# A fp32 hybrid block on one core: the third norm's factor in every eviction of its projection, fewer writes of the normed residual, last projection's residual in two pieces

## The chip, the cores and the metric

One of the cores of one Trainium2 chip runs the whole program. The time is device microseconds (us) from the start to the end of one execution; the median of several executions counts. One execution of the kernel before was profiled, and all rows below come from it.

## What is computed (reference, cut)

A block with T = 512 positions and D = 1024 columns is followed by a second one. The change touches the second, whose middle part is this:

```python
def second_block(x, w_in, norm_g, pool_w, pool_scale, fox_bf, w_out, final_g):
    for layer in range(DEPTH):
        h = rmsnorm_2(x, norm_g[layer])
        z = jnp.einsum('bld,dc->blc', h, w_in[layer])
        (pv, pg, dq, dk, dv, dg, iq, ik, iw, fq, fk, fv, fg, ff) = split_columns(z)
        a_out = pool_mixer(pv, pool_w[layer], pool_scale[layer]) * jax.nn.silu(pg)
        b_o = dsa_mixer(dq..., dk..., dv..., iq..., ik, iw * idx_w_scale, topk)
        b_out = b_o.reshape(B, L, DSA_WIDTH) * jax.nn.silu(dg)
        log_f = jax.nn.log_sigmoid(ff.astype(jnp.float32) + fox_bf[layer].astype(jnp.float32))
        c_o = fox_mixer(fq..., fk..., fv..., log_f)
        c_out = c_o.reshape(B, L, FOX_WIDTH) * jax.nn.silu(fg)
        mixed = jnp.concatenate([a_out, b_out, c_out], axis=-1)
        x = x + jnp.einsum('blc,cd->bld', mixed, w_out[layer])
    return rmsnorm_2(x, final_g)
```

The norm multiplies each column by a gain and each position by one number, r(t). The projection is linear, so r(t) can be multiplied in before it, or after it at each result. The sparse attention (dsa) selects 128 keys per query by scores: eight indexer heads, each relu(iq . ik) times a weight. The forgetting attention (fox) needs the running sum of log f.

## The kernel before, in words

Everything is kept transposed: channels on the 128 partitions, the 512 positions along the row. A projection is a list of **units**. One unit is one block of 128 output columns over all of K = 1024. The fp32 product is made of three passes (high x high, low x high, high x low), so a unit is 8 x 3 = 24 matmuls of 128x512 into one bank of `gb` (four banks, unit u uses u % 4). Its weights arrive by a DMA of SP into `raw` (four buffers), ACT copies them to a rounded `whi` (line 1101), and DVE or POOL subtracts to get `wlo` (line 1494 or 2233). `whi` and `wlo` have two buffers. `split(n)` names this; `POOL_SPLITS` says for which n POOL does the subtraction.

The third stage is a projection of 31 units (`Z_UNITS`), numbered here 0 to 30: unit 0 "thin" (indexer key, indexer weights, forget gates), units 1 and 2 the indexer queries, then q, k, v, g of six head pairs ("groups"), and four units of the pooling mixer. Each engine's program walks these units, four quarters of six matmuls each, and after quarter m of unit u it does what `schedule()` has put at (u, m). Slot s means quarter s % 4 of unit s // 4. In the plan stand, in order of slots: `spread` (PE broadcasts the norm's row r(t) into `gd`, ACT copies it to SBUF), `turn_iw` (PE transposes unit 0's result, DVE takes the gates from it), `log_f` (ACT an exp, DVE a chain of 18 small instructions, each waiting for the one before: `log1p`, line 1499 and after), `cum_f`, `turn_f`, 24 `score` entries (PE one product with 32 rows, ACT relu into one of two buffers, DVE multiply-add into `selb`), 48 `round` entries (DVE max and replace, eight keys each), and for each group the attention steps `s`, `weigh`, `t`, `turn_v`, `pv`, `mix`, `low`.

Before unit 0 the residual in `act_a` is only multiplied by the gain ("raw"): r(t) is not known yet. `RAW_UNITS` = 4 units use this raw residual and get r(t) when DVE evicts them (lines 2035, 2037, 2044). For units 4 to 30 the entries `norm` make a second copy with r(t) in it: DVE eight products (line 1931), ACT eight copies (line 1409), POOL eight subtractions (line 2220). Units from 4 on wait for these by `z_hi` and `z_lo`, and their results are evicted by ACT (q, v, g, pv, pg; lines 1364 to 1386) or DVE (k, line 2046) without a factor. ACT takes the silu of a gate unit straight from PSUM.

All engines work through their own program in order. PE may run at most four banks ahead of evictions, two buffers ahead of splits, and two relu buffers ahead of DVE's scores.

The last projection (`W_ORDER`) has all of `gb` and `gd` as its output, two banks for each of four position tiles c. The residual is put in first as products with the identity (line 1073), for tiles 2, 3, 1, 0, then eight rows of weights follow (line 1086), 24 matmuls each. Tiles 0 and 1 lie in `gb` and may be overwritten only when the last pooled output has been read (`ot_ready` 8).

Of the kernel before, what the change touches and what calls it, by code (L numbers as in the profile page):

```python
# [5 lines left out]
P = 128  # L6
F32 = mybir.dt.float32
# [30 lines left out]
Z_HI, Z_LO = 2 * KD, 3 * KD  # L38
OUT_HI, OUT_LO = 0, KD
RAW_UNITS = 4  # L40
# [32 lines left out]
           + [(w, 0, c) for w, c in (("k", B_FK), ("q", B_FQ), ("v", B_FV), ("g", B_FG))]  # L73
           + [(w, g, c + g * P) for g in range(1, 3) for w, c in (("q", B_FQ), ("k", B_FK), ("v", B_FV), ("g", B_FG))]
# [26 lines left out]


def reads_of(what):
    return [count for (name, _, _), (_, count) in zip(Z_UNITS, Z_READER) if name == what]


Q_READ, K_READ, V_READ, G_READ, PV_READ, PG_READ = (reads_of(w) for w in ("q", "k", "v", "g", "pv", "pg"))


def schedule():  # L110
# [4 lines left out]
    put(1, 2, ("norm", 0))  # L115
    put(2, 0, ("turn_iw",))
    put(2, 1, ("spread", 3))
    put(2, 2, ("norm", 1))
# [4 lines left out]
    for n, (c, h) in enumerate(todo):  # L123
        put((14 + n * 10 // 24) // 4, (14 + n * 10 // 24) % 4, ("score", n, c, h))
# [7 lines left out]
    for g in range(GROUPS):  # L132
        start = 4 * 6 + 16 * g
# [9 lines left out]
        todo.setdefault(start + (7 if g < GROUPS - 1 else 10), []).append((2, ("turn_v", g)))  # L143
# [10 lines left out]
    assert max(todo) == 4 * last  # L154
# [30 lines left out]
def hybrid_block_kernel(nc, x, norm_mix_g, w_in, conv_a_w, gdn_conv_w, gdn_A_log, gdn_dt_bias, gdn_norm_g,  # L185
                        w_a_out, w_b_out, w_o, norm_ffn_g, w_up, ffn_conv_w, w_down, norm_final_g,
                        w_in_2, norm_g_2, pool_w_2, pool_scale_2, fox_bf_2, w_out_2, final_g_2, out):
    with ExitStack() as ctx:
# [109 lines left out]
        token_row, final_row = flat(ob), wk[:, 0:T]  # L298
        fresh = (qc[:], kc[:], vc[:], cx[:], ca[:], flat(LT), flat(AT), flat(Kt))
# [75 lines left out]
        klen_ready = sem("klen_ready")  # L375
        g_kept = sem("g_kept")
# [61 lines left out]
        z_read_v = sem("z_read_v")  # L438
# [52 lines left out]
        POOL_SPLITS = range(N_Z + 5, N_W)  # L491
# [12 lines left out]
        def _(sp):  # L504
# [49 lines left out]
            sp.wait_ge(cols_exp, 2)  # L554
# [62 lines left out]
        def _(pe):  # L617
# [1649 lines left out]
```

## Time and profile before

| | |
|---|---|
| median of 3 runs | 1375.5 us (1375.22 to 1379.77) |
| the profiled execution | 1378.33 us, its span 1376.6 us |
| mean granted TensorE clock over the span | 0.978 |
| busy, share of the span | PE 97%, DVE 60%, ACT 43%, POOL 19% |
| DMA | 113 MB, mean 82 GB/s |

Busy is the time an engine spends in instructions. PE's share says little by itself: a matmul at half clock is busy twice as long. The clock column (PEclk, 1.00 is 2.4 GHz and 0.50 is 1.2 GHz) has to be read beside it. The third stage runs from about 1024 us to 1315 us, the last projection from there to 1370 us.

### The profile page before, as it was taken

The numbers are of one execution on the slowest core, as the hardware profiler recorded it, in microseconds if no ns is written. First come the engines' busy times: TensorE is split into PE (matmuls) and PEld (weight loads), VectorE is DVE, ScalarE is ACT, GpSimd is POOL, SyncE is SP. The second block draws the span as 40 slices with busy tenths as digits, with TensorE's granted clock in tenths as the row PEclk, the third lists the DMA queues.
The fourth block names the chain that finished last, engine by engine and source line by source line (L and its number), as shares of the span: only waits on it lengthen the run. The fifth ranks groups of instructions, "written<-read, shape, count | busy, mean of one in ns | idle before, by whom it ended". The sixth has DMA issues, their size and how long they took to land.

```text
span 1376.6 us, 20315 instructions
## 1 busy us (share of the span) xinstructions
PE 1329.6 (97%) x6848; PEld 1054.3 (77%) x6848; DVE 820.3 (60%) x1685; ACT 588.4 (43%) x1015; POOL 266.6 (19%) x493
## 2 busy tenths in 40 slices
PE   6899999999999999999999999999996999999998
PEld 4788878888788788888788888788775567766676
DVE  4657676666676743345577753677675468873522
ACT  5345445364454432224344432344553255555412
POOL 1113033031230300002400000000134224643200
PEclk9999999999999999999999999999998599999999
DMA  5233232332332223333233233332342122222211
GB/s 157 63 85 85 77 84 76 84 84 69 91 84 72 81 78 92 93 105 92 86 99 100 82 92 107 99 99 75 86 115 64 35 58 62 66 74 62 62 54 69
DMA packets 209560, 113.34 MB, mean 82 GB/s; under 512 B 6954, under 2 KB 206953, under 8 KB 209513
## 3 DMA queue, kind: packets, MB, share of 16 engines
q1 hardware_dynamic: 209129, 112.72, 28.4%
q8 instruction: 26, 0.43, 0.1%
q14 instruction: 21, 0.17, 0.0%
q0 software_dynamic: 384, 0.03, 0.0%
HBM read 110.59 MB, written 2.11 MB: 82 GB/s over the span
## 4 chain that ended last, share of the span: by engine, by line
PE 93%; DVE 4%; ACT 2%; issue 1%; POOL 0%; DMA 0%; POOLq 0%; DVEq 0%; ACTq 0%
PE gb L634 76%; PE gd L1008 2%; PE gb L1086 2%; PE gd L1086 2%; PE gd L979 1%; PE gd L1021 1%; PE gd L1031 1%; PE gd L646 1%; DVE wlo L1494 1%; PE gd L707 1%; PE gd L719 1%; PE gd L811 1%; PE gd L802 0%; PE gb L1073 0%; PE gd L791 0%
## 5 line engine op out<-in xcount | busy, mean ns | idle before, releaser
L634 PE MATMUL gb<-act_a,whi 128*128 128x512 f32 x2800 | 958.8, 404 | 11.8 <-POOL selb L2209 5.0
L634 PEld LDWEIGHTS gb<-act_a,whi 128*128 128x128 f32 x2800 | 531.3, 190 | 141.1 <-issue 19.5
L634 PE MATMUL gb<-act_a,wlo 128*128 128x512 f32 x1488 | 585.3, 393 | 0.0
L1494 DVE TENSOR_TENSOR wlo<-raw,whi 128x1024 fp32r<-128x1024 f32 x186 | 232.3, 1249 | 159.0 <-ACT whi L1101 158.3
L1101 ACT ACTIVATE whi<-raw 128x1024 fp32r<-128x1024 f32 x212 | 224.1, 1057 | 234.6 <-PE gb L634 201.4
L634 PEld LDWEIGHTS gb<-act_a,wlo 128*128 128x128 f32 x1488 | 283.1, 190 | 52.6 <-issue 1.7
L634 PE MATMUL gb<-act_b,whi 128*128 128x512 f32 x304 | 109.2, 389 | 0.0
L2233 POOL TENSOR_TENSOR wlo<-raw,whi 128x1024 fp32r<-128x1024 f32 x26 | 62.8, 2416 | 138.1 <-ACT whi L1101 138.1
L634 PEld LDWEIGHTS gb<-act_b,whi 128*128 128x128 f32 x304 | 57.1, 188 | 11.9
L2199 POOL TENSOR_TENSOR zs<-zs,ca 128x512 f32<-128x512 f32 x3 | 4.4, 1457 | 314.3 <-ACT ca L1104 314.3
L2143 POOL TENSOR_TENSOR elt<-Ti,Ue 128x60 f32<-128x60 f32 (+14 forms) x120 | 44.1, 368 | 27.5 <-POOL Ue L2146 13.3
L2146 POOL TENSOR_TENSOR Ue<-Ue,elt 128x60 f32<-128x60 f32 (+14 forms) x120 | 39.5, 329 | 9.4
L1181 ACT ACTIVATE ob<-gd,hc 128x128 f32<-128x128 f32 x24 | 8.8, 367 | 58.2 <-DVE Rr L1692 58.2
L2171 POOL TENSOR_TENSOR zs<-zs,ca 128x512 f32<-128x512 f32 x3 | 5.6, 1857 | 134.8 <-ACT ca L1104 134.8
L2156 POOL TENSOR_TENSOR rr<-ss,rr 128x4 f32<-128x4 f32 x8 | 1.6, 200 | 152.7 <-DVE ss L1711 152.7
L2150 POOL TENSOR_TENSOR rr<-ss,eps_one 128x4 f32<-128x4 f32 x8 | 2.1, 263 | 142.9 <-DVE ss L1647 142.9
L1873 DVE TENSOR_TENSOR Yb<-gb,Vt 128x512 f32<-128x512 f32 x22 | 15.2, 691 | 23.2 <-PE gb L634 23.2
L1983 DVE MAX8 small<-selb 128x8 f32<-128x256 f32 (+2 forms) x48 | 26.7, 556 | 0.7
L1231 ACT ACTIVATE act_a<-ca 128x512 f32 (+1 forms) x8 | 5.1, 632 | 50.8 <-DVE ca L1758 50.8
L1984 DVE MATCH_REPLACE8 selb<-small,selb 128x256 f32<-128x256 f32 (+2 forms) x48 | 26.1, 543 | 0.0
L634 PE MATMUL gb<-act_b,wlo 128*128 128x512 f32 x64 | 24.9, 389 | 0.0
L1008 PE MATMUL gd<-gate 128*128 128x128 f32 (+7 forms) x96 | 24.8, 459 | 0.0
(458 smaller groups left out, 1593.1 us busy)
## 6 DMA issues: line engine op xcount, KB each, us to landing
raw<-in_w_in_dram SPq DMA_DIRECT2D x103, 512.0 KB, 3.4
raw<-in_w_up_dram SPq DMA_DIRECT2D x44, 512.0 KB, 3.5
raw<-in_w_down_dram SPq DMA_DIRECT2D x16, 384.0 KB, 3.1
raw<-in_w_down_dram SPq DMA_DIRECT2D x16, 320.0 KB, 3.0
raw<-in_w_a_out_dram SPq DMA_DIRECT2D x8, 512.0 KB, 3.4
raw<-in_w_b_out_dram SPq DMA_DIRECT2D x8, 512.0 KB, 3.5
raw<-in_w_o_dram SPq DMA_DIRECT2D x8, 512.0 KB, 3.4
raw<-in_w_out_dram SPq DMA_DIRECT2D x8, 512.0 KB, 3.4
```

Of the source, the lines that this page charges most:

```text
L634: ins = pe.matmul(gb[:, b, :], l, r, start=(first and m == 0), stop=(last and m == len(todo) - 1))
L646: return pe.matmul(gd[:, b, :], ones[:], squares, start=start, stop=stop)
L1008: pe.matmul(gd[:, i, 0:(c + 1) * P], q[r, c * P:c * P + P], ring(g, 2 + i)[r, 0:(c + 1) * P], start=True, stop=True).then_inc(s_done, 1)
L1086: ins = pe.matmul(place(c, half), l, r, start=False, stop=(i == KD - 1 and m == 2), skip_group_check=True)
L1101: sc.activation(whi[:, i % 2, 0:k * P], raw[:, i % 4, 0:k * P], ACT.Copy).then_inc(hi_ready, 1)
L1494: dve.tensor_tensor(wlo[:, i % 2, 0:k * P], raw[:, i % 4, 0:k * P], whi[:, i % 2, 0:k * P].bitcast(F32), ALU.subtract).then_inc(split_read ...
L1873: dve.tensor_tensor(scaled[s], gb[:, 2 * q + s, :], flat(Vt), ALU.mult).then_inc(up_scaled, 1)
L1983: link(dve.max(small[:, 0:8], v))
L1984: link(dve.match_replace(v, small[:, 0:8], v, TAKEN))
L2143: pool.tensor_tensor(elt[:, :, 0:n], row_at(m), Ue[:, :, m:m + 1].to_broadcast([P, TC, n]), ALU.mult).then_inc(el_used, 1)
L2146: pool.tensor_tensor(Ue[:, :, m + 1:E], Ue[:, :, m + 1:E], elt[:, :, 0:n], ALU.subtract).then_inc(el_done, 1)
L2233: pool.tensor_tensor(wlo[:, n % 2, :], raw[:, n % 4, :], whi[:, n % 2, :].bitcast(F32), ALU.subtract).then_inc(split_ready, 1)
```

## The change

1. `norm`, its line 1931, 1409 and 2220 instructions and `RAW_UNITS` are gone. All 31 units read the raw residual. PE has no waits for `z_hi` and `z_lo`.
2. Every unit is evicted by DVE with one `scalar_tensor_tensor` that multiplies by r(t) (`token_row`), and by 0.125 for q. Gates are written to SBUF so, and ACT then takes their silu in place; it waits for DVE's eviction. One semaphore (`z_read`) counts all evictions.
3. The 24 scores are spread over 13 slots, not 10 (slots 14 to 26). The groups of attention start at slot 28 + 15 g, not 24 + 16 g. The four units of group 0 come as q, k, v, g.
4. POOL subtracts from weight block 9 of the stage on, not 5; blocks 5 to 8 are DVE's. POOL's transfers of the forget rows of groups 0 and 1 stand ahead of its first subtraction.
5. PE waits for POOL's memsets (`pads_ready`) before unit 4, not before unit 1.
6. The copies of the indexer key (`ik4`) move on ACT from `spread` to `turn_iw`.
7. In the last projection PE does residual 2 and 3, the first row of weights for tiles 2 and 3, then residual 1 and 0 and the rest of the first row.
8. The results of the last mixer go to other slots of `act_a` (`MIX_HI`, `MIX_LO`), since the raw residual now stays. In the first block, one semaphore of the decay rows is split in three; nothing is reordered there.

```diff
-RAW_UNITS = 4
...
-           + [(w, 0, c) for w, c in (("k", B_FK), ("q", B_FQ), ("v", B_FV), ("g", B_FG))]
-           + [(w, g, c + g * P) for g in range(1, 3) for w, c in (("q", B_FQ), ("k", B_FK), ("v", B_FV), ("g", B_FG))]
+           + [(w, g, c + g * P) for g in range(3) for w, c in (("q", B_FQ), ("k", B_FK), ("v", B_FV), ("g", B_FG))]
...
     put(1, 2, ("spread", 2))
-    put(1, 2, ("norm", 0))
-    put(2, 0, ("turn_iw",))
-    put(2, 1, ("spread", 3))
-    put(2, 2, ("norm", 1))
+    put(2, 1, ("turn_iw",))
+    put(2, 2, ("spread", 3))
     put(3, 1, ("log_f",))
...
-        put((14 + n * 10 // 24) // 4, (14 + n * 10 // 24) % 4, ("score", n, c, h))
+        put((14 + n * 13 // 24) // 4, (14 + n * 13 // 24) % 4, ("score", n, c, h))
...
-        start = 4 * 6 + 16 * g
+        start = 4 * 7 + 15 * g
...
-        POOL_SPLITS = range(N_Z + 5, N_W)
+        POOL_SPLITS = range(N_Z + 9, N_W)
...
-                if u == 1:
+                if u == 4:
                     pe.wait_ge(pads_ready, 1)
...
+            residual(2)
+            residual(3)
+            pe.wait_ge(split_ready, N_W + 1)
+            pe.wait_ge(m_lo, 1)
+            products(0, 2)
+            products(0, 3)
+            residual(1)
+            residual(0)
+            products(0, 0)
+            products(0, 1).then_inc(unit_done, 1)
...
+                if what in ("g", "pg"):
+                    sc.wait_ge(z_read, u + 1)
+                    sc.activation(sg[g % 2][:], sg[g % 2][:], ACT.Silu).then_inc(gate_silu, 1)
...
+                def scale(dst, rows=slice(0, P), factor=1.0):
+                    return dve.scalar_tensor_tensor(dst[rows, :], src[rows, :], factor, token_row[rows, :], ALU.mult, ALU.mult)
...
+            pool.wait_ge(f_rows, 1)
+            decay_rows(0)
+            decay_rows(1)
             pool.wait_ge(xrb_kept, 1)
             pool.wait_ge(split_ready, POOL_SPLITS[0])
             for n in POOL_SPLITS:
-                if n == N_Z + 7:
-                    pool.wait_ge(f_rows, 1)
-                    decay_rows(0)
-                    decay_rows(1)
```

**DVE, units 3 and 4**, from the end of the log of the forget gates. L1970 and L1973 are scores (two relu buffers, `Yb` and `zs`), L2044 the eviction of unit 3. Before:

```order
L1953 MEMSET sm 128x6 [waits dve_order]
L1955 TENSOR_TENSOR sm<-sm 128x6 [waits dve_order] x3
L1970 TENSOR_SCALAR selb<-Yb,sm 128x256 [waits relu_ready]
L1973 SCALAR_TENSOR_TENSOR selb<-zs,sm,selb 128x256 [waits relu_used,relu_ready]
L1973 SCALAR_TENSOR_TENSOR selb<-Yb,sm,selb 128x256 [waits relu_used,relu_ready]
L1973 SCALAR_TENSOR_TENSOR selb<-zs,sm,selb 128x256 [waits relu_used,relu_ready]
L1973 SCALAR_TENSOR_TENSOR selb<-Yb,sm,selb 128x256 [waits relu_used,relu_ready]
L1973 SCALAR_TENSOR_TENSOR selb<-zs,sm,selb 128x256 [waits relu_used,relu_ready]
L1973 SCALAR_TENSOR_TENSOR selb<-Yb,sm,selb 128x256 [waits relu_used,relu_ready]
L1973 SCALAR_TENSOR_TENSOR selb<-zs,sm,selb 128x256 [waits relu_used,relu_ready]
L1978 MEMSET selb 64x64 [waits relu_used]
L2044 TENSOR_TENSOR gate<-gb,ob 64x512 [waits unit_done,dve_order]
```

With the change (here L1922 and L1925 are the scores, L1453 is `wlo` of weight block 5, L1990 an eviction):

```order
L1905 MEMSET sm 128x6 [waits dve_order]
L1907 TENSOR_TENSOR sm<-sm 128x6 [waits dve_order] x3
L1922 TENSOR_SCALAR selb<-Yb,sm 128x256 [waits relu_ready]
L1925 SCALAR_TENSOR_TENSOR selb<-zs,sm,selb 128x256 [waits relu_used,relu_ready]
L1925 SCALAR_TENSOR_TENSOR selb<-Yb,sm,selb 128x256 [waits relu_used,relu_ready]
L1925 SCALAR_TENSOR_TENSOR selb<-zs,sm,selb 128x256 [waits relu_used,relu_ready]
L1453 TENSOR_TENSOR wlo<-raw,whi 128x1024 [waits hi_ready]
L1925 SCALAR_TENSOR_TENSOR selb<-Yb,sm,selb 128x256 [waits relu_used,relu_ready]
L1925 SCALAR_TENSOR_TENSOR selb<-zs,sm,selb 128x256 [waits relu_used,relu_ready]
L1990 SCALAR_TENSOR_TENSOR gate<-gb,wk 64x512 [waits pads_ready,unit_done]
```

The low part of weight block 5, which POOL did, now stands on DVE behind the log and the first four scores. Unit 5 (counted from 0) needs it; the split of block 4 stands ahead of the log in both. Before, eight scores stood in a row ahead of the eviction of unit 3; now four, the split, two and then that eviction.

**PE, the start of the last projection.** L1073 is the residual by the identity, L1086 the products with the first row of weights. Before:

```order
L1073 MATMUL gd<-ident,xT 128x128 [waits exp_ready,xT_norm]
L1073 MATMUL gd<-ident,xT 128x128 x7
L1073 MATMUL gd<-ident,xT 128x128 [waits ot_ready]
L1073 MATMUL gd<-ident,xT 128x128 x7
L1073 MATMUL gb<-ident,xT 128x128 [waits ot_ready]
L1073 MATMUL gb<-ident,xT 128x128 x7
L1073 MATMUL gb<-ident,xT 128x128 [waits ot_ready]
L1073 MATMUL gb<-ident,xT 128x128 x7
L1086 MATMUL gb<-whi,act_a 128x512 [waits m_lo,split_ready]
L1086 MATMUL gb<-whi,act_a 128x512
```

With the change (L1048 and L1059 are the same two lines; the first residual tile stands just ahead):

```order
L1048 MATMUL gd<-ident,xT 128x128 [waits ot_ready]
L1048 MATMUL gd<-ident,xT 128x128 x7
L1059 MATMUL gd<-whi,act_a 128x512 [waits m_lo,split_ready]
L1059 MATMUL gd<-whi,act_a 128x512
L1059 MATMUL gd<-wlo,act_a 128x512
L1059 MATMUL gd<-whi,act_a 128x512 x2
L1059 MATMUL gd<-wlo,act_a 128x512
L1059 MATMUL gd<-whi,act_a 128x512 x2
L1059 MATMUL gd<-wlo,act_a 128x512
L1059 MATMUL gd<-whi,act_a 128x512 x2
L1059 MATMUL gd<-wlo,act_a 128x512
L1048 MATMUL gb<-ident,xT 128x128 [waits ot_ready]
```

Half of the first row of weights, for the tiles in `gd`, now stands ahead of the wait for `ot_ready`.

## Rows read from the trace of the kernel before

**Rows 1.** The page, chain of waits that ended last, by engine.

```profile
PE 93%; DVE 4%; ACT 2%; issue 1%; POOL 0%; DMA 0%; POOLq 0%; DVEq 0%; ACTq 0%
```

**Rows 2.** Busy time of each engine in stretches: from:to, length, busy (instructions), PEclk, DMA.

```profile
1071.00:1082.00 11.00, 10.38 (x26) 6.02 (x26) 5.25 (x19) 3.03 (x7) 2.34 (x1) 0.50 0.17 47
1093.00:1115.00 22.00, 20.45 (x64) 10.27 (x64) 10.34 (x22) 10.06 (x18) 6.45 (x9) 0.77 0.10 25
1150.00:1183.00 33.00, 32.49 (x156) 23.96 (x154) 27.27 (x79) 18.52 (x43) 18.33 (x11) 1.00 0.23 65
```

**Rows 3.** Timeline of PE: start, us, engine, line, operation, tiles [idle before, releaser].

```profile
1041.06 0.79 PE L634 MATMUL gb<-act_a,whi 128*128 128x512 f32 x1 [4.98 <-POOL selb L2209]
...
1057.08 0.50 PE L634 MATMUL gb<-act_a,whi 128*128 128x512 f32 x1 [0.63 <-DVE wlo L1494]
...
1067.80 1.40 PE L979 MATMUL gd<-dec,KT 32*128 32x256 f32 x4 [6.35 <-DVE QT L2037]
```

**Rows 4.** Chain of waits in order of time: start us, us, what.

```profile
1041.06 6.26 PE gb L634 x18
...
1073.63 1.16 PE gd L979 x4
...
1074.78 2.86 PE gb L634 x6
...
1083.46 1.58 PE gd L979 x4
...
1093.02 0.89 PE gd L979 x4
...
1103.24 1.11 PE gd L979 x4
...
1115.12 5.49 PE gb L634 x24
```

**Rows 5.** Timeline of DVE, around the log of the forget gates and the scores.

```profile
1065.36 1.79 DVE L1494 TENSOR_TENSOR wlo<-raw,whi 128x1024 fp32r<-128x1024 f32 x1 [1.64 <-ACT whi L1101]
...
1067.07 0.68 DVE L2037 TENSOR_TENSOR QT<-gb,ob 128x512 f32<-128x512 f32 x1
...
1067.67 0.64 DVE L1499 TENSOR_SCALAR sm<-sm 128x24 f32<-128x24 f32 x1
...
1072.53 0.35 DVE L1970 TENSOR_SCALAR selb<-Yb,sm 128x256 f32<-128x256 f32 x1
...
1073.59 0.48 DVE L1973 SCALAR_TENSOR_TENSOR selb<-Yb,sm,selb 128x256 f32<-128x256 f32 x1
...
1105.07 0.75 DVE L1973 SCALAR_TENSOR_TENSOR selb<-zs,sm,selb 128x512 f32<-128x512 f32 x1 [2.32 <-issue]
...
1105.93 0.75 DVE L1973 SCALAR_TENSOR_TENSOR selb<-Yb,sm,selb 128x512 f32<-128x512 f32 x1
```

**Rows 6.** The page, costliest groups: line engine op tiles xcount | busy, mean ns | idle.

```profile
L1494 DVE TENSOR_TENSOR wlo<-raw,whi 128x1024 fp32r<-128x1024 f32 x186 | 232.3, 1249 | 159.0 <-ACT whi L1101 158.3
...
L1101 ACT ACTIVATE whi<-raw 128x1024 fp32r<-128x1024 f32 x212 | 224.1, 1057 | 234.6 <-PE gb L634 201.4
```

**Rows 7.** Groups by form, 1105 to 1321 us, DVE and ACT, same columns.

```profile
L1984 DVE MATCH_REPLACE8 selb<-small,selb 128x384 f32<-128x384 f32 x16 | 8.7, 543 | 0.0
...
L1983 DVE MAX8 small<-selb 128x8 f32<-128x384 f32 x16 | 8.9, 556 | 0.3
...
L2077 DVE SCALAR_TENSOR_TENSOR ca<-gb,par,vc 128x512 f32<-128x512 f32 x1 | 0.8, 751 | 0.1
...
L1372 ACT ACTIVATE vraw<-gb 128x512 f32<-128x512 f32 x6 | 3.6, 595 | 0.0
```

**Rows 8.** Timeline of PE and DVE at the start of the last projection.

```profile
1315.15 3.84 PE L1073 MATMUL gd<-ident,xT 128*128 128x128 f32 x32
...
1321.13 5.47 PE L1073 MATMUL gb<-ident,xT 128*128 128x128 f32 x32 [2.14 <-DVE ca L2077]
...
1320.33 0.75 DVE L2077 SCALAR_TENSOR_TENSOR ca<-gb,par,cx 128x512 f32<-128x512 f32 x1
```

More of the change, by code:

```diff
@@ L153, in schedule @@
             put(slot // 4, slot % 4, e)
-    assert max(todo) == 4 * last
+    assert max(todo) <= 4 * last
     return at
@@ L1043, in _ @@
                 if u >= 4:
-                    reader, count = Z_READER[u - 4]
-                    pe.wait_ge({"act": z_read, "dve": z_read_v}[reader], count)
-                if u == 1:
+                    pe.wait_ge(z_read, u - 3)
+                if u == 4:
                     pe.wait_ge(pads_ready, 1)
-                p = unit(N_Z + u, N_Z + u, u % 4, 0, H_HI if u < RAW_UNITS else Z_HI, H_LO if u < RAW_UNITS else Z_LO,
-                         parts=4, ready=(h_ready, 2 * KD) if u == 0 else (z_lo, 0) if u == RAW_UNITS else None,
-                         high=(hn_hi, 2 * KD) if u == 0 else (z_hi, 0) if u == RAW_UNITS else None)
+                p = unit(N_Z + u, N_Z + u, u % 4, 0, H_HI, H_LO, parts=4,
+                         ready=(h_ready, 2 * KD) if u == 0 else None, high=(hn_hi, 2 * KD) if u == 0 else None)
                 for m in range(4):
@@ L1066, in _, with residual @@
             pe.wait_ge(xT_norm, KD)
-            for c in (2, 3, 1, 0):
+            def residual(c):
                 pe.wait_ge(*((ot_ready, GROUPS + 2), (ot_ready, GROUPS + 2), (exp_ready, TC * 2 * GROUPS),
@@ L1405, in beside @@
                         sc.activation(final_row, gd[:, 1, :], ACT.Copy).then_inc(xrb_kept, 1)
-                elif what == "norm":
-                    for k in range(4 * e[1], 4 * e[1] + 4):
-                        sc.wait_ge(zn_ready, k + 1)
-                        sc.activation(act_a[:, Z_HI + k, :], fresh[k], ACT.Copy).then_inc(z_hi, 1)
+                elif what == "turn_iw":
+                    sc.wait_ge(z_read, 1)
+                    for i in range(4):
+                        ins = sc.activation(ik4[32 * i:32 * i + 32, :], flat(iwff)[0:32, :], ACT.Copy)
+                    ins.then_inc(ik_ready, 1)
                 elif what == "log_f":
@@ L2040, in z_out @@
                         dve.wait_ge(s_done, TC * 2 * (g - 1))
-                    for i in range(2):
-                        r = slice(64 * i, 64 * i + 64)
-                        if u < RAW_UNITS:
-                            ins = dve.tensor_tensor(ring(g, 2 + i)[r, :], gb[r, u % 4, :], token_row[r, :], ALU.mult)
-                        else:
-                            ins = dve.tensor_copy(ring(g, 2 + i)[r, :], gb[r, u % 4, :])
-                    ins.then_inc(z_read_v, 1)
+                    for i, r in enumerate(halves):
+                        ins = scale(ring(g, 2 + i), r)
+                elif what == "q" and g < 3:
+                    if g == 2:
+                        dve.wait_ge(s_done, TC * 2)
+                    for i, r in enumerate(halves):
+                        ins = scale(ring(g, i), r, 0.125)
+                elif what == "q":
+                    dve.wait_ge(s_done, TC * 2 * (g - 1))
+                    ins = scale(ring(g, 0), factor=0.125)
+                elif what == "v":
+                    if g:
+                        dve.wait_ge(v_turn_done, g)
+                    ins = scale(vraw)
+                elif what in ("g", "pg"):
+                    n = g if what == "g" else GROUPS + g
+                    if n >= 2:
+                        dve.wait_ge(ot_ready, n - 1)
+                    ins = scale(sg[g % 2])
+                elif what == "pv":
+                    if g:
+                        dve.wait_ge(win_ready, 1)
+                    ins = scale(pvb)
+                ins.then_inc(z_read, 1)
             def windows(g):
@@ L2084, in _ @@
                 for m in range(4):
-                    if m == 1 and u and u != 2:
+                    if m == 1 and u:
                         z_out(u - 1)
@@ L2088, in _ @@
                         beside(e)
+            z_out(len(Z_UNITS) - 1)
             for e in plan[(len(Z_UNITS), 0)]:
```

149 lines of the change are left out of this document (48 added, 101 removed).

## The prediction, before the change was run

> **What bounds the kernel now.** I read the chain of waits first: PE holds 93% of it [rows 1], so an edit pays only where PE waits or runs slowly. Next the table of stretches, for the clock beside PE's busy time. From 1071 to 1082 us PE is busy 10.38 of 11.00 us at a granted clock of 0.50, the 1.2 GHz level, and from 1093 to 1115 at 0.77; from 1150 to 1183 it is busy 32.49 of 33.00 at 1.00 [rows 2]. So the loss in the third stage lies between 1036 and 1115 us, in two forms. The timeline of PE shows the first: idle 4.98 us ahead of unit 1, released by POOL's memset; 0.63 ahead of unit 3; 6.35 ahead of the first score, released by DVE's eviction of unit 2 [rows 3]. The chain in order of time shows the second: six matmuls of a unit take 2.86 us at 1074.78, and 24 take 5.49 at 1115.12, which is 1.37 for six; 18 take 6.26 right after the first wait, where 4.12 would do [rows 4]. The reader should see that PE is counted busy there and does half the work. Then DVE: 27.27 of 33.00 us from 1150 to 1183 [rows 2], the engine that this change loads.
>
> Numbers are made against the profiled execution (1378.33 us, its span 1376.6), which is 2.8 us above the median of 1375.5. I take the gain from the median.
>
> **Term 1, up to the first score.** The memsets are waited for ahead of unit 4, and they end long before it: 4.98 goes. Without the second copy (eight products on DVE, eight copies on ACT, eight subtractions on POOL) nothing stands between DVE and the splits and evictions of units 1 to 3: 0.63 and 6.35 go. Without the first wait the clock has no reason to fall there: 6.26 - 4.12 = 2.14 goes. Together 14.1, so the first score moves from 1067.80 [rows 3] to 1053.7. Is something late next? Unit 3 would start 4.1 earlier, at 1049.6; behind it ACT's high part 1.06, DVE's low part 1.25 [rows 6] and the eviction of unit 2 at 0.75 (the same form as [rows 7], 751 ns) end at 1052.7. That is covered by 1 us, no more. Gain **14.1**.
>
> **Term 2, the scores, to the start of unit 7.** Before, 1067.80 to 1119.24 (1115.12 plus 18 of 24 matmuls), 51.4 us. Work of PE with the change, at full clock: 13 quarters at 1.37 = 17.8; scores in pairs, of 384 0.89 and of 512 1.11; of 256 only the low level has a row, 1.16, and with the ratio of the 384 (1.58 to 0.89) that is 0.65 [rows 4]; four pairs of each, 10.6; the matmuls of the forget gates some 1.3. Sum 29.7. DVE: the log chain takes 1067.67 to 1072.53 = 4.86 [rows 5] and starts at 1052.7, so the first score is used from 1057.6. Then 24 scores at 0.53 (256; two from 1072.53 to 1073.59), 0.86 (512; start to start) and 0.7 between them [rows 5] = 16.7; evictions of units 3, 4 (two halves, 1.5 each) and 5, 3.75; low parts of blocks 5, 6 and 7, 3.75; seven rounds, narrower than those of 384 at 556 + 543 ns [rows 7], 1.0 each; copies 0.4. Sum 31.6, so DVE ends unit 6's share at 1089.2. PE may be only three scores ahead: score 4 needs relu 2, and relu 2 needs DVE's use of score 0, done at 1058.1, so PE, at slot 16 by 1057.9, gets both its scores off by 1059.6, 1.2 us late. Going on so, slot by slot, I get 0.2 to 0.5 us at three later ones, and unit 7 at 1085.5. The low part of block 5, moved behind the log and four scores, ends near 1061.4; PE wants it for unit 5 at 1066: covered, by 5 us. Ends: all at full clock with no waits, 1083.4; all at the low level, 13 x 2.86 + 4 x (1.16 + 1.58 + 1.97) + 1.9 = 57.9, 1111.6. I take 1088, near the first end, because the wait of 6.35 us ahead of the low stretch is gone and no slot has three scores any more (before, four of ten had), and add 2.5 for one fall of the clock at slot 16. Gain 1119.2 - 1088 = **31.2, of which 14.1 is term 1**, so 17.1 here. The first attention pair, done in unit 6 before, comes after: -0.4.
>
> **Term 3, units 7 to 30.** PE's work is the same. DVE gets q, v and g of each group: 1.5 + 0.75 + 0.75, and 0.1 on k, 3.1 us per four units, on top of 27.3 per 33 [rows 2]: 92%. ACT loses 0.6 per piece [rows 7], which pays nothing, as it is not waited for. While rounds last (to slot 82, in unit 20) DVE has little slack, and it enters unit 7 some 4 us behind PE. All of DVE's new work there, 9 us of evictions and a low part of 1.25, plus that lag, would be -15; none is 0. I take **-5**, nearer to 0, since each group's chain (s, exp, weigh, t) has three to five slots of 1.4 us or more, and DVE's new sum stays under PE's. Groups start every 15 slots, not 16: same work, and it ends one slot earlier. ACT's silu now waits for DVE, and the exponentials are queued behind it; that is in the 5. POOL's subtractions cost PE nothing while DVE's low parts at 1.25 replace POOL's; its transfers of the forget rows start right after `f_rows`, some 15 us ahead of their use.
>
> The moved work has a price that depends on the engine: the same 512 from PSUM take 595 ns on ACT and 751 on DVE [rows 7]. The Trainium skill (VectorE: DVE Perf Modes, the section on the TRN2 errata) gives 120 + 512 cycles at 0.96 GHz for DVE and 172 + 512 at 1.2 GHz for ACT, an estimate of 658 and 570 ns; by it the 12 evictions in term 3's bound would cost 1.1 us less, and the sum would be 0.4 better.
>
> One low part on DVE took 1.79 while POOL worked [rows 5], against 1.25 on the mean [rows 6]. If evictions were held like that, 0.54 more for some 17 pieces up to unit 20, term 3 would be 9 us worse. The Trainium skill (SBUF — State Buffer, its part on the shared port pair) says that a VectorE instruction with at most one SBUF input does not contend with GpSimd; an eviction reads one operand in PSUM, so by that rule the 9 us are not there. No row of mine shows such an eviction beside POOL, so the 9 stays as part of a rival.
>
> **Term 4, the last projection.** Before, PE did two residual tiles in 3.84, stood 2.14 and did the other two in 5.47, at the low level [rows 8]. Now 12 matmuls of the first weight row (2.75) fill the wait. The last pooled result, at 1320.33 + 0.75 before, comes 0.75 later, since DVE's eviction of unit 30 stands in its chain: 1321.83, and PE is ready at 1315.15 + 3.84 + 2.75 = 1321.74. Then 3.84 + 2.75 end at 1328.4; before, the first row ended at 1321.13 + 5.23 + 5.49 = 1331.85. Gain **3.4**.
>
> **Sum:** 14.1 + 17.1 - 0.4 - 5 + 3.4 = 29.2, from 1375.5: **1346.3 us**.
>
> **Rivals.** (a) The clock stays low through the scores. For: from 1071 to 1082 PE was 94% busy and still at 0.50 [rows 2]; scores use 32 rows. Against: two scores per slot, not up to three, and no long wait ahead. Unit 7 at 1105, between the ends: 17 us less, 1363.5. (b) DVE bounds units 7 to 20: term 3 is -15, 1356.5; with the hold beside POOL as well, 1365. For: 92%, in order, waits inside. (c) Slower than before: DVE is late at unit after unit, and PE, with gaps between, drops to 1.2 GHz in the units of rounds and attention. Price 4 x (2.86 - 1.37) = 6 us a unit; it turns the sign from the fifth unit, and from the seventh it is slower by over 0.5%. Nine units, 7 to 15, would give 1400. Against: before, DVE was at 83% there and the clock at 1.00. (d) The waits only move: the first score comes no earlier than ACT's exp and DVE's log allow, and the time lost in term 2 grows by what term 1 gave; 1373.
>
> **How the numbers follow.** Forecast 0.66 (1338 to 1355), (a) 0.15, (b) 0.13, (c) 0.03, (d) 0.03. The low end is 1083.4 in term 2 and half of term 3's loss: 29.2 + 4.6 + 2.5 = 36, 1339, and 1338 for the bounds of small terms. The high end reaches to (a) less its worst part, 1362. About 0.5% is what a measurement of this kernel can tell from no change: 6.9 us. Below 1368.6 lie the forecast, (b) and nearly all of (a): 0.92; (d) and the rest of (a) give 0.05; (c) 0.03.
>
> **What would show it.** PE without idle time ahead of unit 1 and a granted clock of 1.00 from 1036 to 1056; first score near 1054; short idle times ahead of slot 16, released by ACT's relu; unit 7 near 1088; DVE above 90% from there to some 1180; PE idle in sum 5 us more than before in units 7 to 20, released by DVE; between residual tiles no gap over 0.3 us. The prediction is wrong if the clock is 0.50 through units 4 to 6, if PE waits for a low part of blocks 5 to 8, or if DVE's evictions cost more than 0.8 us each.

## The result, and the profile after

The changed kernel takes **1344.7 us** (median of 4 runs, 1344.17 to 1345.51), the kernel before 1375.65 beside it (1375.22 to 1379.77): ratio **0.9769**, 95% interval 0.975 to 0.9788, so 31 us faster. 1346.3 us was forecast. The profiled execution took 1345.02 us, its span is 1343.3.

The page gives the chain of waits by engine, to be held against [rows 1]:

```profile
PE 90%; DVE 7%; issue 1%; ACT 1%; DMA 0%; POOL 0%; DVEq 0%; POOLq 0%; ACTq 0%
```

PE is still the bound, but DVE's share has grown from 4 to 7%. Busy time in stretches of the changed kernel (columns as in [rows 2]):

```profile
1036.00:1048.00 12.00, 12.00 (x62) 10.11 (x60) 6.16 (x12) 5.13 (x7) 3.77 (x7) 1.00 0.56 161
...
1071.00:1082.00 11.00, 11.00 (x45) 5.61 (x43) 9.90 (x23) 4.99 (x9) 3.70 (x8) 1.00 0.20 51
...
1093.00:1115.00 22.00, 21.24 (x92) 15.41 (x91) 21.03 (x55) 10.75 (x25) 7.22 (x3) 1.00 0.31 87
1115.00:1148.00 33.00, 30.36 (x145) 22.61 (x146) 27.86 (x80) 16.40 (x42) 14.71 (x11) 1.00 0.18 50
1148.00:1181.00 33.00, 32.09 (x155) 23.73 (x154) 30.86 (x74) 16.62 (x42) 21.65 (x13) 1.00 0.23 64
```

The clock is 1.00 (the 2.4 GHz level) in all of them, where it was 0.50 from 1071 to 1082 and 0.77 from 1093 to 1115 [rows 2]. DVE is busy 21.03 of 22 us in the third. The chain in order of time, at the scores (to be held against [rows 4]) and in the last projection:

```profile
1054.32 0.63 PE gd L957 x4
1054.95 1.58 PE gb L613 x6
...
1058.75 0.99 PE gd L957 x4
1059.74 1.58 PE gb L613 x6
...
1292.17 3.84 PE gb L1048 x32
1296.01 5.49 PE gb L1059 x24
```

Six matmuls behind a pair of scores take 1.58 us: not the 2.86 of the kernel before, and not the 1.37 of the forecast either. Where the 33.3 us between the two profiled spans came from:

| Stretch | before | after | gain | forecast |
|---|---|---|---|---|
| to the first score | 1067.80 | 1054.26 | 13.5 | 14.1 |
| from there to unit 7 | 51.4 | 32.8 | 18.6 | 17.1 |
| from there to the first residual tile | 195.9 | 198.3 | -2.4 | -5.4 |
| last projection and end | 61.5 | 57.9 | 3.6 | 3.4 |

The execution profiled before lay 2.8 us above its median, the one after 0.3. So the rows hold 2.3 us more than the 31 between the medians, and in some row the gain is smaller than it looks. The trace can't say in which.

### The profile page after: what moved, and what is told of

It is laid out like the page before. It is cut to its first block, busy times and chain, and to the rows that moved or that the text cites. A ratio compares the mean times of both kernels' runs of the same rounds, so it can differ in the third digit from the quotient of the medians.

```text
span 1343.3 us, 20290 instructions
## 1 busy us (share of the span) xinstructions
PE 1312.0 (98%) x6848; PEld 1044.0 (78%) x6848; DVE 839.4 (62%) x1706; ACT 574.0 (43%) x990; POOL 244.5 (18%) x481
## 4 chain that ended last, share of the span: by engine, by line
PE 90%; DVE 7%; issue 1%; ACT 1%; DMA 0%; POOL 0%; DVEq 0%; POOLq 0%; ACTq 0%
PE gb L613 75%; PE gb L1059 2%; PE gd L1059 1%; PE gd L985 1%; PE gd L1008 1%; PE gd L998 1%; PE gd L625 1%; PE gd L957 1%; PE gd L686 1%; PE gd L698 1%; PE gd L790 1%; DVE selb L1936 1%; PE gd L781 1%; DVE wlo L1453 0%; DVE small L1935 0%
## 5 line engine op out<-in xcount | busy, mean ns | idle before, releaser
L1453 DVE TENSOR_TENSOR wlo<-raw,whi 128x1024 fp32r<-128x1024 f32 x190 | 236.7, 1246 | 155.4 <-ACT whi L1091 154.7
L2205 POOL TENSOR_TENSOR wlo<-raw,whi 128x1024 fp32r<-128x1024 f32 x22 | 53.1, 2412 | 120.3 <-ACT whi L1091 120.3
L2120 POOL TENSOR_TENSOR elt<-Ti,Ue 128x60 f32<-128x60 f32 (+14 forms) x120 | 43.3, 361 | 27.1 <-POOL Ue L2123 13.3
```

What stands on the lines that cost most here:

```text
L1453: dve.tensor_tensor(wlo[:, i % 2, 0:k * P], raw[:, i % 4, 0:k * P], whi[:, i % 2, 0:k * P].bitcast(F32), ALU.subtract).then_inc(split_read ...
L2120: pool.tensor_tensor(elt[:, :, 0:n], row_at(m), Ue[:, :, m:m + 1].to_broadcast([P, TC, n]), ALU.mult).then_inc(el_used, 1)
L2205: pool.tensor_tensor(wlo[:, n % 2, :], raw[:, n % 4, :], whi[:, n % 2, :].bitcast(F32), ALU.subtract).then_inc(split_ready, 1)
```

## The experiments

Each kernel ran beside the kernel before on the same chip. Costs below are differences of these ratios times 1375.5 us, so that the drift of a chip drops out. The interval of a ratio is 0.16 to 0.24% to either side, 2 to 3 us, so a difference of two ratios is known to some 3 to 4 us. A cost of 4 to 6 us is leaned on only where the trace shows as much.

### The parts, taken back one at a time

```diff
-                if u == 4:
+                if u == 1:
                     pe.wait_ge(pads_ready, 1)
```

> The changed kernel with one line back: PE waits for the POOL memsets ahead of unit 1 and not ahead of unit 4. My theory (waits and the low clock behind them are paid one by one): an idle time of some 5.0 us ahead of unit 1, the 1.2 GHz level for some 7 us behind it at a price of 2.1 us, the scores still at the 2.4 GHz level, 7.1 us in all: 1351.8 us. Rival 1 (one fall brings the next): the clock is low again through the scores as in the kernel before, 1.37 to 2.86 us per six matmuls: 1369 us. Rival 2 (the work behind has slack): DVE, 4 to 8 us ahead of PE's scores, takes up part of the wait: 1348 us.

Measured: 1351.3 us, ratio 0.982 (0.9804 to 0.9836), a cost of 7.0 us. PE's timeline, and a stretch:

```profile
1041.30 0.79 PE L613 MATMUL gb<-act_a,whi 128*128 128x512 f32 x1 [4.98 <-POOL selb L2186]
```

```profile
1040.00:1048.00 8.00, 6.71 (x24) 5.44 (x25) 0.00 (x0) 0.00 (x0) 0.97 (x4) 0.66 0.49 139
...
1060.00:1071.00 11.00, 11.00 (x52) 6.92 (x50) 9.50 (x31) 3.59 (x9) 0.00 (x0) 1.00 0.36 95
```

The wait and the low clock behind it are back; the scores stay at 1.00. The first theory holds: this term adds by itself.

```diff
-        put((14 + n * 13 // 24) // 4, (14 + n * 13 // 24) % 4, ("score", n, c, h))
+        put((14 + n * 10 // 24) // 4, (14 + n * 10 // 24) % 4, ("score", n, c, h))
```

> The changed kernel with the 24 scores over 10 slots again (two or three a slot), attention where the change has it. My theory (the wait of 6.35 us ahead of the first score made the clock fall, not how close the scores stand): clock 1.00 through the scores, DVE has to use 2.4 scores a slot and PE waits 0 to 2 us for it: 1344 to 1347 us. Rival (slots with three scores of 32 rows let the clock fall): 0.50 somewhere between 1060 and 1085 us and 10 to 17 us more: 1355 to 1362 us.

Measured: 1351.1 us, ratio 0.9812 (0.9795 to 0.983), 5.9 us. The waits of PE by releaser (total, times, longest), then two stretches:

```profile
PE gd L957 <- ACT zs L1381: 1.5, 2, 0.8
PE gd L957 <- ACT Yb L1381: 1.3, 2, 0.7
```

```profile
1075.00:1080.00 5.00, 4.17 (x15) 1.64 (x12) 4.04 (x10) 2.48 (x6) 4.09 (x8) 1.00 0.43 111
1080.00:1085.00 5.00, 5.00 (x13) 2.52 (x13) 2.80 (x7) 1.36 (x3) 0.00 (x0) 0.60 0.01 1
```

My theory falls. A third score in a slot waits for ACT's relu of the first, four times 0.56 to 0.83 us, and with no long wait anywhere the clock goes to the 1.2 GHz level behind the last two. The four waits are 2.8 us, and from 1081.0 to 1087.8 PE is busy throughout at the low level, which costs it 3.4: 6.2 for the 5.9 measured. So the scores at ten slots bring a fall of their own. One of the four runs took 1347.45 us, the others, one of them profiled, 1350.8 and more.

The last projection in the old order (all four residual tiles, then the first weight row whole):

```diff
             residual(3)
+            residual(1)
+            residual(0)
...
-            residual(1)
-            residual(0)
```

> The changed kernel with the last projection in the order of the kernel before: all four residual tiles, then the first weight row whole. My theory: PE stands some 2.7 us between the second and the third residual tile (3.84 + 2.72 us of matmuls no longer lie there), and runs at the 1.2 GHz level behind it at a price of 1.6 us: 1344.7 + 2.5 + 1.6 = 1348.8 us. Rival 1 (no fall of the clock this time): 1347.2 us. Rival 2 (the order does nothing, the time is set by the transfers of the weight rows): 1344.7 us.

Measured: 1349.3 us, ratio 0.9804 (0.9788 to 0.9821), 4.8 us. PE's timeline:

```profile
1292.66 5.47 PE L1048 MATMUL gb<-ident,xT 128*128 128x128 f32 x32 [2.93 <-DVE ca L2052]
```

In the changed kernel the same tiles read

```profile
1285.40 3.84 PE L1048 MATMUL gd<-ident,xT 128*128 128x128 f32 x32
...
1292.17 3.84 PE L1048 MATMUL gb<-ident,xT 128*128 128x128 f32 x32 [0.15 <-DVE ca L2053]
```

The wait is 2.93 in place of 0.15, and 5.47 in place of 3.84 is the low level: 2.78 + 1.63 = 4.4 of the 4.8 us.

The raw residual can't be taken back by one line. So the kernel before was given the three other parts:

```diff
-                if u == 1:
+                if u == 4:
                     pe.wait_ge(pads_ready, 1)
...
-        put((14 + n * 10 // 24) // 4, (14 + n * 10 // 24) % 4, ("score", n, c, h))
+        put((14 + n * 13 // 24) // 4, (14 + n * 13 // 24) % 4, ("score", n, c, h))
...
-        start = 4 * 6 + 16 * g
+        start = 4 * 7 + 15 * g
...
-        todo.setdefault(start + (7 if g < GROUPS - 1 else 10), []).append((2, ("turn_v", g)))
+        todo.setdefault(start + (7 if g < GROUPS - 1 else 11), []).append((2, ("turn_v", g)))
```

and the last projection of the changed kernel. It lacks the raw residual with its evictions on DVE, and also items 4 and 6 of the change and the new order of group 0, which no run tried by themselves.

> The kernel before with three parts of the change: the wait for the memsets ahead of unit 4, the scores over 13 slots with attention from slot 28, and the last projection's residual in two pieces. What is missing is the raw residual: the second normalized copy stays, with the wait ahead of the first score, and DVE has no evictions of q, v and g. Theory 1 (the raw residual is worth the wait ahead of the first score, 6.4 us with 5 to 7 us of low clock behind it, less what DVE's load costs, 2.5 us): 1344.7 + 9 to 11 = 1354 to 1356 us. Theory 2 (the added load on DVE eats the gain): 1345 to 1348 us. Theory 3 (it takes the raw residual to keep the clock up): 1362 us.

Measured: 1350.4 us, ratio 0.9806 (0.9789 to 0.9822): the raw residual, with these smaller items, is worth 5.1 us, between the first theory and the second. Its timeline, a stretch of its later units, and PE's waits ahead of the transposes of the probabilities (here L1021):

```profile
1061.38 1.43 PE L979 MATMUL gd<-dec,KT 32*128 32x256 f32 x4 [6.35 <-DVE QT L2052]
```

```profile
1148.00:1181.00 33.00, 32.25 (x155) 24.07 (x154) 29.84 (x73) 17.31 (x41) 22.20 (x13) 1.00 0.25 65
```

```profile
PE gd L1021 <- DVE zs L2024: 1.6, 2, 0.8
PE gd L1021 <- issue: 1.5, 3, 1.0
```

The first score is 7.1 us later than in the changed kernel, the last pair of scores 9.2 (1093.76 to 1084.61). But from there to the first residual tile it needs 197.2 us, the changed kernel 200.8. The raw residual gains 9.2 and gives 3.6 back. The waits ahead of the transposes are 3.1 us here and 6.4 in the changed kernel (its rows stand below, with the run of the half rounds), which is 3.3 of the 3.6.

### Parts put into the kernel before alone

The scores' spread alone (13 slots, attention from slot 28 every 15):

> The kernel before with one part of the change alone: the 24 scores over 13 slots, attention from slot 28 every 15 slots. The waits ahead of unit 1 (4.98) and ahead of the first score (6.35) stay. Theory 1 (the long wait brings the low level, the spread of the scores sets how long it lasts): clock 0.50 for some 12 us behind the first score and then 1.00, against 27 us and two shorter stretches before: 9 to 14 us faster, 1362 to 1366 us. Theory 2 (the wait alone decides): low level through the scores as before, 0 to 3 us faster, 1373 to 1376 us. Theory 3 (attention begun later is lost time): slower than before by 2 to 4 us.

Measured: 1360.8 us, ratio 0.9887 (0.9871 to 0.9904): 15.5 us faster, 1.5 more than any theory gave. Both long waits stand; three stretches:

```profile
1066.00:1070.00 4.00, 3.19 (x8) 2.17 (x9) 3.58 (x15) 0.66 (x2) 1.28 (x1) 0.50 0.50 131
1070.00:1075.00 5.00, 5.00 (x21) 2.93 (x20) 3.34 (x14) 2.37 (x5) 0.97 (x1) 0.84 0.00 0
1075.00:1080.00 5.00, 5.00 (x26) 3.30 (x25) 4.64 (x8) 1.47 (x4) 1.42 (x1) 1.00 0.40 105
```

The low level ends near 1071 us, where the kernel before has it to 1092.9, with two shorter stretches behind. Around the scores it lasts 6.8 us (1064.8 to 1071.6) with PE busy for 4.8 of them, before 37.6 us with PE busy for 34.4; work at half the clock takes twice as long, so half of the busy time is the price: 2.4 us in place of 17.2. The edit does more than spread the scores, though, since the attention begins later with it: PE's waits ahead of the transposes of the probabilities fall from 4.5 to 3.3 us, and one of 0.6 ahead of a transpose of the values is gone. So are the four short waits inside the scores (2.6 us). Together 19.2, for the 18.9 us between the two profiled executions; some 1.8 of it belongs to the later attention and not to the scores.

The wait for the memsets alone:

> The kernel before with PE's wait for the memsets ahead of unit 4 in place of unit 1, nothing else. Theory 1 (terms add): units 1 to 3, the sums' spread and all that DVE and ACT hang on them come 4.98 + 2.14 = 7.1 us earlier, the wait ahead of the first score stays at some 6.4: 1368.4 us. Theory 2 (the second normalized copy on DVE, ACT and POOL is what the first score waits for, and it can't start earlier, so that the wait moves): 1374 to 1376 us.

Measured: 1368.9 us, ratio 0.9944 (0.9928 to 0.9961): 7.7 us faster, the first theory: the terms add. Its profiled execution took 1363.75 us, though, the three others 1368.3 to 1369.7. In the profiled one the low level ended at some 1077 us, after 17 us, and was not followed by the two shorter stretches:

```profile
1070.00:1075.00 5.00, 4.38 (x12) 2.27 (x10) 1.85 (x4) 1.78 (x4) 2.35 (x1) 0.50 0.04 4
1075.00:1080.00 5.00, 5.00 (x16) 3.10 (x16) 2.41 (x6) 1.26 (x3) 0.00 (x0) 0.71 0.36 101
1080.00:1085.00 5.00, 4.28 (x22) 2.48 (x21) 2.29 (x5) 1.66 (x4) 0.00 (x0) 1.00 0.00 2
```

The order of instructions through the scores is that of the kernel before. The mean granted clock was 0.986 in the profiled execution and 0.981 to 0.982 in the three slower ones. So how long the low level lasts in ten-slot scores differs between executions of one program.

### Does the long wait bring the low clock, and what keeps it?

PE waits ahead of the first score for a chain of POOL memsets behind DVE's log (`held` is a new semaphore):

```diff
+                    if n == 0:
+                        pe.wait_ge(held, 1)
...
+            pool.wait_ge(f_ready, 1)
+            for _ in range(6):
+                link(pool.memset(cbias[:, 0:T - P], 0.0))
+            pool.memset(cbias[:, 0:T - P], 0.0).then_inc(held, 1)
```

> The changed kernel with a wait ahead of the first score: PE waits there for POOL, which waits for DVE's log of the forget gates and then does seven memsets, so that PE stands some 6 us, as in the kernel before (6.35). Nothing else is added on DVE. My theory (the wait is what brings the low level, and scores keep it there): granted clock 0.50 through most of the scores, 6 us of idle time and 12 to 20 us of low clock, 1362 to 1371 us. Rival 1 (the clock comes back within some 7 us, as behind the wait ahead of unit 1 in the kernel before): 6 + 2 us, 1353 us. Rival 2 (nothing but the wait): 1351 us.

Measured: 1354.6 us, ratio 0.9844 (0.9827 to 0.986), 10.3 us. PE's timeline, and stretches:

```profile
1060.69 1.31 PE L960 MATMUL gd<-dec,KT 32*128 32x256 f32 x4 [6.79 <-POOL cbias L2201]
```

```profile
1066.00:1070.00 4.00, 4.00 (x13) 2.31 (x11) 2.19 (x3) 1.60 (x3) 0.00 (x0) 0.51 0.00 0
1070.00:1075.00 5.00, 5.00 (x27) 3.31 (x25) 3.52 (x8) 1.32 (x4) 0.00 (x0) 1.00 0.38 105
```

The wait does bring the 1.2 GHz level, from 1056.3 us, inside the wait, to 1069.9: it ends within 10 us of the first score although scores stand in the slots. That is rival 1 with 2 us more. Both edits in one:

> Both edits of the two runs before in one: the changed kernel with the wait of some 6.8 us ahead of the first score, and with the scores over 10 slots. Alone they cost 6.4 us (four waits of 0.56 to 0.83 us ahead of third scores, a stretch at 0.50 to 0.60 near 1080) and 9.9 us (the wait, and 1.2 GHz for some 12 us behind it). Theory 1 (it takes both: the long wait brings the 1.2 GHz level, and the short waits of the three-score slots bring it again or keep it): more than the sum, granted clock 0.50 through nearly all of the scores, as in the kernel before: 1344.7 + 22 to 26 = 1367 to 1371 us. Theory 2 (the costs simply add): 1361 us. Theory 3 (they overlap, since DVE catches up while PE stands): 1355 to 1358 us.

Measured: 1360.5 us, ratio 0.9873 (0.9856 to 0.9891), 14.3 us against 10.3 + 5.9 = 16.2. Theory 1 falls. The cost is nearer to the second theory (they add) than to the third (10.3 to 13.3), but the interval does not separate the two. The low level, which theory 1 wanted through nearly all of the scores, goes from 1056.4 to 1076.9: 20.5 us, which is the 13.6 of the wait alone and the 6.8 of the ten slots alone. No run showed why the kernel before held it to 1093.

### DVE's load in units 7 to 30

Every eviction of units 7 to 30 done twice:

```diff
+                    if u >= 7:
+                        link(dve.scalar_tensor_tensor(dst[rows, :], src[rows, :], factor, token_row[rows, :], ALU.mult, ALU.mult))
```

> The changed kernel with every eviction of units 7 to 30 done twice on DVE: 31 more instructions at 0.69 us, 21 us over some 200. Theory 1 (after the change DVE has little left up to slot 82: busy 30.86 of 33 us from 1148 to 1181): with 3.5 us more per 33 it is over the full time there, and PE waits 5 to 13 us more, 1350 to 1358 us. Theory 2 (DVE's evictions still lie beside PE's work, and the added load of the change was free): under 1.5 us, 1345 to 1346 us.

Measured: 1353.7 us, ratio 0.9837 (0.9814 to 0.9861), 9.4 us for 21 us of added work, the first theory. PE's waits ahead of the transposes (L998) rose from 6.4 to 12.4 us. Next, every second round left out, so that the selection keeps half its positions and the result is not the block's (24 rounds, by the rows 8 x (0.85 + 1.10 + 1.37) = 26.6 us and not the 21 of the expectation):

```diff
-                    link(dve.max(small[:, 0:8], v))
-                    link(dve.match_replace(v, small[:, 0:8], v, TAKEN))
+                    if r % 2 == 0:
+                        link(dve.max(small[:, 0:8], v))
+                        link(dve.match_replace(v, small[:, 0:8], v, TAKEN))
```

> The changed kernel with every second round of the selection left out (24 of 48; the selection keeps half its positions, so the output of the indexed heads differs): some 21 us less on DVE between units 5 and 20. Theory 1 (the 6.4 us that PE stands ahead of the transposes of the probabilities in units 7 to 30 come of DVE's load, as does the 4 us by which the kernel with raw residual loses to the one without in these units): most of it goes up to unit 21, 1339 to 1341 us. Theory 2 (the waits are the length of the chain score, minimum, exp, reciprocal, product, and not the load): 1343 to 1345 us.

Measured: 1338.0 us, ratio 0.9724 (0.97 to 0.9748), 6.2 us faster, a little past the first theory. PE's waits ahead of the same transposes, first of the changed kernel, then of this one:

```profile
PE gd L998 <- issue: 3.9, 6, 1.2
PE gd L998 <- DVE zs L1961: 1.5, 2, 0.8
PE gd L998 <- DVE Yb L1961: 1.0, 2, 0.8
```

```profile
PE gd L998 <- DVE Yb L1962: 0.8, 1, 0.8
PE gd L998 <- issue: 0.5, 1, 0.5
```

6.4 us of waits became 1.3. So they come of DVE's load, not of the chain's length alone. But DVE is not always the last link. The rows with "issue" have no releaser by the profile; the engine to look at is ACT. In the changed kernel:

```profile
1120.10 1.05 ACT L1091 ACTIVATE whi<-raw 128x1024 fp32r<-128x1024 f32 x1
1121.17 1.28 ACT L1348 ACT_TABLE_LOAD   x1
1122.46 0.63 ACT L1348 ACTIVATE cx<-cx 128x512 f32<-128x512 f32 x1
1123.00 0.58 ACT L1407 ACTIVATE pT<-gd 128x512 f32<-128x512 f32 x1
```

```profile
1123.68 0.63 PE L998 MATMUL gd<-ident,zs 128*128 128x128 f32 x4 [1.15 <-issue]
```

PE starts 0.1 us after ACT's copy of the transposes before, whose bank it needs again (the kernel has PE wait there for `pT_ready`, which that copy sets). So it is at the five others, 1106.76, 1115.58, 1140.48, 1180.02 and 1262.96. Here the copy stood behind a high part, a table load and the silu of a gate. DVE gives the probabilities late, so the transposes come late, and ACT's queue is then in other work. The same waits from the other side, the transposes one slot later:

```diff
-                todo.setdefault(start + 4 * c + 5 + t % 2, []).append((0, ("t", c, t)))
+                todo.setdefault(start + 4 * c + (6 if c < 3 else 5) + t % 2, []).append((0, ("t", c, t)))
...
-        todo.setdefault(start + (7 if g < GROUPS - 1 else 11), []).append((2, ("turn_v", g)))
+        todo.setdefault(start + (8 if g < GROUPS - 1 else 12), []).append((2, ("turn_v", g)))
```

> The changed kernel with the transposes of the probabilities one slot later for the first three query blocks of a pair (slots 6 and 7 behind the start of the block in place of 5 and 6), and the transposes of the values one slot later with them. No instruction is added. If the waits ahead of these transposes (6.4 us in sum) are a chain that is one slot short, some 4 us go: 1340 to 1342 us. If DVE is simply behind and works its queue off, the wait moves to the next transposes or ahead of the sums with the values: 1343 to 1345 us. If ACT's copies of the last transposes now end after the sums are due: 1346 us or more.

Measured: **1341.0 us** (1340.57 to 1341.71), ratio 0.9742 (0.9719 to 0.9765), 3.7 us faster than the changed kernel: the best version here that computes the whole block. The intervals of the two ratios overlap a little; but each of its four times lies below each of the changed kernel's (1344.17 to 1345.51), and from the last scores to the first residual tile its trace needs 197.1 us, 3.7 fewer than 200.8. The waits fall from 6.4 to 4.3 us; where the other 1.6 comes from was not looked for. What is left:

```profile
PE gd L998 <- issue: 3.5, 2, 2.1
PE gd L998 <- DVE Yb L1961: 0.8, 1, 0.8
```

A last version on top of it, meant to take those too:

```diff
-        POOL_SPLITS = range(N_Z + 9, N_W)
+        POOL_SPLITS = range(N_Z + 7, N_W)
...
-        put((20 + n * 62 // 47) // 4, (20 + n * 62 // 47) % 4, ("round", r, c))
+        put((24 + n * 58 // 47) // 4, (24 + n * 58 // 47) % 4, ("round", r, c))
```

> The kernel with late transposes (1341.0 us) and two edits that take work off DVE between slots 20 and 40: POOL makes the low parts of blocks 7 and 8 as well (2.5 us less on DVE), and the 48 rounds of the selection are spread over slots 24 to 82 in place of 20 to 82 (1 to 3 rounds fewer are due at any slot up to 45, some 2 us). If the two or three waits left at 1119 to 1123 us (0.80, 1.43 and what belongs to 3.5 in sum) are DVE's arrears from the scores: 1337 to 1339.5 us. If POOL's low parts (2.4 us each, and DVE's products of two SBUF operands slower beside them: 1.5 to 2.5 us in place of 0.35 to 0.5) cost what they give: 1340 to 1342 us. If POOL comes late for block 7 behind its transfers of the forget rows, PE stands ahead of unit 7: 1343 us or more.

Measured: 1347.0 us, ratio 0.9784 (0.9766 to 0.9801), 5.8 us slower than without these two edits; the third case by its size, but by another path, as PE does not stand ahead of unit 7. POOL, DVE, ACT and PE in its timeline:

```profile
1119.74 2.36 POOL L2205 TENSOR_TENSOR wlo<-raw,whi 128x1024 fp32r<-128x1024 f32 x1 [9.14 <-ACT whi L1091]
```

```profile
1118.18 0.49 DVE L1961 TENSOR_SCALAR Yb<-Yb,small 128x512 f32<-128x512 f32 x1
...
1120.03 2.35 DVE L1961 TENSOR_SCALAR zs<-zs,small 128x512 f32<-128x512 f32 x1
```

```profile
1123.02 0.63 ACT L1348 ACTIVATE cx<-cx 128x512 f32<-128x512 f32 x1 [2.05 <-DVE cx L1990]
1123.55 0.58 ACT L1407 ACTIVATE pT<-gd 128x512 f32<-128x512 f32 x1
```

```profile
1124.23 1.08 PE L998 MATMUL gd<-ident,zs 128*128 128x128 f32 x4 [3.48 <-issue]
```

The product of the probabilities takes 0.49 us alone and 2.35 when POOL's low part starts just ahead of it. The eviction of the gate `cx` is queued behind it on DVE, ACT's silu waits 2.05 us for that eviction, ACT's copy for the silu, and PE 3.48 us for the copy; the next six matmuls take 2.51 in the chain, nearly all at the low level. In sum PE waits 8.5 us ahead of transposes here and 4.3 without the two edits, and 3.4 us lie at the low level, 1.7 more: 5.9 for the 5.8. The kernel without the two edits has the same low part, at 1120.22, but there the product had begun at 1119.26 and took 0.48: a small shift in time decides whether the two meet. Which of the two edits is to blame more was not separated.

## Why the prediction was right, and where it was not

**Term 1** was right: forecast 14.1, measured 13.5 between the traces; first score at 1054.26 for a forecast 1053.7, no idle time ahead of units 1 and 3. The run with the memset wait puts 7.0 on the first part (7.1 forecast).

**Term 2** was right in size (18.6 for 17.1) and wrong in two of its steps. First, PE's own work: I took 13 quarters at 1.37 us, but behind a score they take 1.58, 2.7 us more. PE stood nowhere, so its work alone makes unit 7 start at 1087.1 where I had 1085.5 with waits. The short wait ahead of slot 16 did not come, nor the fall of the clock for which I added 2.5; the errors cancel, 1087.1 against 1088. That the size came out is in this part luck. (The kernel before has two such quarters at full clock in its chain, 1.60 at 1110.43 and 1.59 at 1113.09, so the 1.58 could have been read.)

Secondly the reason. I gave the missing wait of 6.35 us as the first ground for the high clock. The runs say that a long wait costs its length and 2.0 to 3.5 us more (4.98 cost 7.0, 6.79 cost 10.3), and that the spread of the scores is the larger part: 15.5 us put in alone with the later attention, while the ten-slot scores fall to the low level with no long wait at all.

The parts taken back one by one cost 7.0 + 5.9 + 5.1 + 4.8 = 22.8 of 31.8 us (2.31% of 1375.5). Four costs, each known to some 3 to 4 us, do not by themselves prove that the other 9 are real, but they fit the one pair that can be compared: the spread is worth 15.5 us where the waits stand (some 1.8 of it for the later attention, which the other run leaves in place) and 5.9 where they are gone.

**Term 3** was right in sign and nearer to 0, as argued: -2.4 between the two traces, -3.6 against the kernel that keeps the second copy (its measure of DVE's load alone), -5.4 forecast with the first pair's 0.4. The kernel before had waits of its own ahead of these transposes, which I had not set off:

```profile
PE gd L1021 <- issue: 4.5, 7, 1.4
```

So PE's waits there rose from 4.5 to 6.4 us, not by the 5 us of the prediction's last part: the later attention took 1.2 to 1.4 of them away (3.3 and 3.1 us in the two runs with it and without the load) and DVE's load added 3.3. The mechanism holds: 21 us more on DVE cost 9.4, some 26 less give 6.2. How much of a wait a given load would bring was chosen in the forecast, between 0 and 15, and not worked out; the nearness to -5 is no proof of it. But "ACT loses 0.6 per piece, which pays nothing, as it is not waited for" was wrong: 3.9 of the 6.4 us end with a copy on ACT that stands behind a silu, an exp or a high part. DVE was over 90% from 1093 to 1115 and from 1148 to 1181, but 27.86 of 33 between.

An eviction took 0.67 to 0.69 us, not the 0.75 that I took from the row with a factor per partition. And q comes in two halves only up to group 2; from group 3 it is one instruction, so DVE's new load is some 2.1 us per four units there and not 3.1.

**Term 4** was right: 3.6 for 3.4, the wait 0.15.

**Rivals.** (a) did not happen with 13 slots; the ten-slot run shows that it was a real risk of the kernel's older table, at 5.9 us and not 17. (b) had the right engine at a sixth of the price. The hold beside POOL never fell on an eviction, see below. (c) and (d) did not happen. The prices of (a) and (b) are 0.2 us above what their own words add up to, and the 1373 of (d) does not follow from its sentence, by which it would be 1346.3 + 14.1 = 1360.4. The median lies 1.6 us below the forecast.

## To carry to other kernels

Look for the low clock before waits: a stretch with PE over 90% busy at the 1.2 GHz level can hold more time than all idle rows, and spreading small products so that none of them waits can be worth more than removing the long wait ahead of them. When DVE is over 90% busy, ask where in its queue the product stands that PE wants next; one slot more between producer and use gave back here about what the added load had cost. Keep the wanted product away from a large POOL instruction, and where a wait has no releaser in the profile, look at which engine's instruction ends just ahead of its end.

## What was not expected of the hardware

**DVE beside POOL.** In the changed kernel, around 1155 us:

```profile
1153.60 2.46 DVE L1961 TENSOR_SCALAR zs<-zs,small 128x512 f32<-128x512 f32 x1
...
1155.98 0.55 DVE L1935 MAX8 small<-selb 128x8 f32<-128x384 f32 x1
...
1157.62 0.67 DVE L1990 SCALAR_TENSOR_TENSOR vc<-gb,wk 128x512 f32<-128x512 f32 x1
```

POOL was busy through all three, with a low part from 1153.40 for 2.38 us and products of the residual behind it. The product of the probabilities, from SBUF to SBUF, took 2.46 us for 0.49 alone; the eviction and MAX8 took what they take alone. So it is in all of units 7 to 30: evictions of 128x512 take 0.67 to 0.69 beside POOL as without it, `low` (two SBUF operands) 0.69 alone and up to 2.72 beside it. The held product ends 0.28 us behind the end of POOL's low part. The one at 1271.33, which began 0.06 us ahead of such a low part, took 0.49, so in these cases it counted which of the two began first. The Trainium skill (SBUF — State Buffer, the part on the shared port pair) has this: a VectorE instruction with two SBUF inputs, beside a GpSimd instruction that reads SBUF, or one in a two-port mode such as tensor_scalar can enter, may be blocked for the whole GpSimd instruction; one with at most one SBUF input and outside these modes is not. The trace agrees: 2.46 beside POOL against 0.49 alone for the product, 0.67 beside it against 0.68 alone for the eviction. The prediction gives only the half of it that clears the evictions, and leaves out the clause on the two-port modes; the products of the probabilities fall under that clause, and the last run fell over one of them.

**The quarter behind a score.** Six matmuls of 128 rows take 1.58 us behind a pair of 32-row products and 1.37 to 1.40 behind the transposes, at the same granted clock of 1.00. The nine quarters behind scores that stand in the chain of the changed kernel take 1.58 to 1.60 each. It is not the scores alone: behind the sums with the values, whose products fill 64 columns of the array (`128*64` in the trace), six matmuls take 1.59 at 1130.36 and 1.61 at 1162.83. The trace does not say why.
